# Attention scores from a head's own 64 rows in place of queries widened with zeros to 128 rows

## The chip, the cores and the metric

The kernel runs on one core of one Trainium2 chip. Its time is the device time of one execution in microseconds (us). The core has five engines that run side by side and wait for each other by semaphores: TensorE (PE, matrix products; its loads of stationary weights are listed apart as PEld), VectorE (DVE), ScalarE (ACT), GpSimd (POOL) and SyncE (SP, here only DMA issues).

## The reference

Two transformer blocks over 512 tokens of width 1024 are followed by a third block with a recurrence (RWKV-7) beside a convolution. The change touches only the attention of the first two. Every layer has 12 token heads and 4 memory heads of 64 channels:

```python
def windowed_gqa(q, k, v, sink, t5_table):       # layer 0: 12 query heads, 4 key heads
    ...
        s = jnp.einsum('bqkgd,bskd->bkgqs', q_blk, k_blk,
                       preferred_element_type=jnp.float32) * scale + bias
        s = jnp.where(valid, s, NEG)
        p = jax.nn.softmax(jnp.concatenate([s, sink_l], axis=-1), axis=-1)[..., :SPAN]
        return jnp.einsum('bkgqs,bskd->bqkgd', p.astype(v_blk.dtype), v_blk)

def neighbourhood_attn(q, k, v, rpb):            # layer 1: 12 heads on an 8x64 grid
    ...
        s = jnp.einsum('bwhd,brwchd->bhwrc', q_row, k_nb,
                       preferred_element_type=jnp.float32) * scale + bias
        p = jax.nn.softmax(s.reshape(B, B_HEADS, GRID_W, kr * kc), axis=-1)
        ...
        return jnp.einsum('bhwrc,brwchd->bwhd', p, v_nb)

def memory_attn(q, mk, mv):                      # both layers: 4 heads, 256 memory rows
    s = jnp.einsum('bshd,bmhd->bhsm', q, mk, preferred_element_type=jnp.float32) * (HEAD_DIM ** -0.5)
    p = jax.nn.softmax(s, axis=-1).astype(mv.dtype)
    return jnp.einsum('bhsm,bmhd->bshd', p, mv).reshape(B, S, MEM_HEADS * HEAD_DIM)
```

So each score is a sum over the 64 channels of one head. Layer 0 also takes a sink value per head into the softmax.

## The kernel before

All activations lie with channels on the 128 partitions (rows) and tokens along the free axis. A row tile of queries or keys holds two heads: one on rows 0 to 63, the other on rows 64 to 127. `qT` holds the token queries in 6 tiles, `kT` the keys, `qmT` the memory queries in 2 tiles, `mkT` the memory keys.

The program is written out engine by engine. Every engine runs its own list in order. For a dense layer ("project"), SyncE loads a panel of weights, ScalarE rounds it (w_hi, line L745), GpSimd forms the rest (w_lo, L602), and TensorE takes three passes per chunk of 128 channels (L1704, L1705, L1706). Two panels are in hand at a time. GpSimd's list has the two first panels of the output projection ahead of its work for attention (`split_lo(L["qm0"].p1 + 2)`, L607, and the same for layer 1 at L652).

Attention of one layer is 64 units: 8 tiles of two heads (the last two tiles are memory heads), times the two heads (e), times 4 blocks of 128 queries. A unit's keys are 128 x 2 or 3 wide in layer 0 (256 or 384), 192 or 256 in layer 1, and 256 for memory. For unit i:

- TensorE computes the score into PSUM (L1741): the stationary operand is the unit's queries, the moving one its keys. Both are fp32, and the trace shows two passes for such a product. It has to wait for the row maximum three units back.
- VectorE adds the bias (L1303) and takes the row maximum (L1309; L1300 without bias). In layer 0 GpSimd has put the sink beside the scores (`put_sink`, L619), and the maximum waits for it.
- ScalarE takes the exponential with its sum (L880).
- TensorE transposes the result (L1750), ScalarE copies that to pT (L854, L857), and TensorE multiplies it with the values (L1761, "PV").
- After 8 units the tile is normalised (L1283, L1284), turned to channels (L1727) and split for the output projection (L865, L1290).

TensorE's list interleaves these: score of unit i, transposes of unit i - 3, PV of unit i - 4, and so on. In layer 1 the windows of values are shifted by 64 keys, so that the first window of block 0 and the last of block 3 have 64 rows only (`pT[0:m, ...]` with m = 64); the trace shows their weights as `64*128`. The other weights of this loop have 128 rows, and a transpose with 64 columns appears as `128*64`.

The score of one head must not see the other head's rows. For that, GpSimd makes for every tile and both heads a copy of the 512 queries on 128 rows, the other head's rows multiplied by zero (`widen`, L621 to L626; the factor is a column of `head_ones`). The copies lie in `q_wide`, in the place of h_hi and h_lo. GpSimd widens tile t just before the sinks of tile t's units. The score of a tile's first unit waits for `q_wide_ready` (L1740).

Of the kernel before, what the change touches and what calls it, by code (L numbers as in the profile page):

```python
# [5 lines left out]
P = 128  # L6
D = 1024
KD = D // P
TOK = 512
NT = TOK // P  # L10
HD = 64
# [94 lines left out]
def build(nc, t, out, scratch):  # L106
# [4 lines left out]
    with ctx:  # L111
# [4 lines left out]
        sg = Signals()  # L116
# [59 lines left out]
        qT = at("qT", [P, 6, TOK], big)  # L176
        kT = at("kT", [P, 6, TOK], big + 12288)

        q_wide = at("q_wide", [P, 2, KD, TOK], h_off)
        qmT = at("qmT", [P, 2, TOK], big + 24576)  # L180
        vtok = at("vtok", [P, 5, HEADS * HD], big + 28672)
        bias_a = at("bias_a", [P, HEADS, SPAN_A], big + 44032)
# [130 lines left out]
        L = {}  # L313
# [21 lines left out]
        def units(layer):  # L335
            lst = []
            for tile in range(8):
                for e in range(2):
                    for blk in range(NT):
                        u = {"tile": tile, "e": e, "blk": blk, "sink": None, "bias": None}  # L340
                        u["q"] = q_wide[:, e, tile, blk * P:blk * P + P]
                        if tile >= 6:
                            b = 64 * e
                            u["from"] = (e, qmT[:, tile - 6, :])
                            u["k"] = mkT[:, layer, tile - 6, :]
                            u["w"] = MEM
                            vc = ((tile - 6) * 2 + e) * HD
                            u["v"] = [(i * P, P, mv[:, layer, i, vc:vc + HD]) for i in range(2)]
                        elif layer == 0:
                            head = 2 * tile + e  # L350
                            par, i = (head // 3) % 2, (head // 6) * 3 + head % 3
                            b = 64 * par
                            lo_k, hi_k = max(0, blk - 1), min(NT, blk + 2)
                            u["from"] = (par, qT[:, i, :])
                            u["k"] = kT[:, i // 3, lo_k * P:hi_k * P]
                            u["w"] = (hi_k - lo_k) * P
                            c0 = (lo_k - blk + 1) * P
                            u["bias"] = bias_a[:, head, c0:c0 + u["w"]]
                            u["sink"] = sinks[:, head:head + 1]
                            vc = (head // 3) * HD  # L360
                            u["v"] = [((i2 - lo_k) * P, P, vtok[:, i2, vc:vc + HD]) for i2 in range(lo_k, hi_k)]
                        else:
                            head = 2 * tile + e
                            b = 64 * e
                            s0, s1 = max(0, P * blk - 64), min(TOK, P * blk + 192)
                            u["from"] = (e, qT[:, tile, :])
                            u["k"] = kT[:, tile, s0:s1]
                            u["w"] = s1 - s0
                            c0 = s0 - (P * blk - 64)
                            ty = 0 if blk == 0 else (2 if blk == NT - 1 else 1)  # L370
                            u["bias"] = bias_b[:, head, ty, c0:c0 + u["w"]]
                            vc = head * HD
                            u["v"] = []
                            for w in (blk, blk + 1):
                                w0 = max(0, 128 * w - 64)
                                n = min(TOK, 128 * w + 64) - w0
                                u["v"].append((w0 - s0, n, vtok[0:n, w, vc:vc + HD]))
                        lst.append(u)
            return lst
# [202 lines left out]
        def _(pool):  # L582
# [26 lines left out]
            def attention(layer):  # L609
# [8 lines left out]
                        w = ul[i]["w"]  # L618
                        nc.gpsimd.tensor_copy(score[:, i % 4, w:w + 1], ul[i]["sink"]).then_inc(sg["sink_put"], 1)  # L619

                def widen(tile):  # L621

                    for e in range(2):
                        b, src = ul[8 * tile + 4 * e]["from"]
                        ins = nc.gpsimd.tensor_scalar(q_wide[:, e, tile, :], src, head_ones[:, 64 * b:64 * b + 1], None, ALU.mult)  # L625
                    ins.then_inc(sg["q_wide_ready"], 1)  # L626

                pool.wait_ge(used, last_reader[2 if layer == 0 else 5])
                for g in range(L[f"qm{layer}"].g0 + L[f"qm{layer}"].groups - 4, L[f"qm{layer}"].g0 + L[f"qm{layer}"].groups):
                    freed(pool, g)  # L630
                for i in range(NU):
                    if i % 8 == 0:
                        widen(i // 8)
                    put_sink(i)

            added = [0]
# [986 lines left out]
        def _(pe):  # L1623
# [92 lines left out]
            def attention(layer):  # L1716
# [15 lines left out]
                for i in range(NU + 4):  # L1732
                    if i < NU:
                        u = ul[i]
                        if i >= 3:
                            pe.wait_ge(sg["max_done"], b0 + i - 2)
                            if ul[i - 3]["bias"] is None:
                                pe.wait_ge(sg["exp_done"], b0 + i - 2)
                        if i % 8 == 0:
                            pe.wait_ge(sg["q_wide_ready"], 8 * layer + u["tile"] + 1)  # L1740
                        nc.tensor.matmul(ps[:, i % 3, 0:u["w"]], u["q"], u["k"], start=True, stop=True  # L1741
                                         ).then_inc(sg["s_done"], 1)
                    k = i - 3
# [415 lines left out]
```

## Time and profile before

| | us |
|---|---|
| median of 3 runs | 2575.73 (2573.24 to 2575.99) |
| profiled execution | 2571.74 |
| its span, first to last instruction | 2569.9 |
| TensorE busy | 2397.3 (93%) |
| ScalarE, VectorE, GpSimd busy | 901.2, 1022.1, 1031.3 |
| mean granted TensorE clock | 0.967 of 2.4 GHz |

A clock of 1.00 is 2.4 GHz, and 0.50 is the lower level, 1.2 GHz. Durations of matmuls include the time that a pass is under way inside the array, so that consecutive passes overlap in the trace; the distance between two starts tells the pace. Attention of layer 0 lies at about 146 to 256 us of the span and that of layer 1 at about 812 to 920 us. The transposes and products named above are all in these stretches.

### The profile page before, as it was taken

The page shows a single profiled execution, that of the slowest core. Times are in us where ns is not written, and L with a number is a line of the kernel's source. Part 1 is how long each engine was busy: PE and PEld are TensorE (multiplying, and loading weights), DVE is VectorE, ACT ScalarE, POOL GpSimd, SP SyncE. Part 2 cuts the span into 40 slices and gives each one's busy share as a digit, 9 for nine tenths or more (in the row PEclk, how much of TensorE's full clock was granted, in tenths as well). Part 3 has the DMA queues.
Part 4 walks back from the last instruction along what each step waited for, and adds up shares of the span by engine and source line. Part 5 has one row for each costly group of instructions (what it writes and reads, how often), then busy time and mean ns, then how long its engine had stood idle before and what let it go on. Part 6 is the DMA issues. An engine that isn't in the chain of part 4 may idle for free.

```text
span 2569.9 us, 41460 instructions
## 1 busy us (share of the span) xinstructions
PE 2397.3 (93%) x17520; PEld 1996.1 (78%) x17520; DVE 1022.1 (40%) x1492; ACT 901.2 (35%) x1519; POOL 1031.3 (40%) x594
## 2 busy tenths in 40 slices
PE   6889899999898989999988999999899998999998
PEld 6767678888687877888866888786888876788886
DVE  3246432221436643222125898437434445322212
ACT  3346433322413733222223222355233334332222
POOL 2342444444546044444454444434200244444444
PEclk9999999999899989999989999999899998999999
DMA  6510233333342022333333333322000222233332
GB/s 158 119 42 1 66 106 99 99 93 97 84 112 71 1 66 74 98 95 92 97 86 102 99 98 94 112 86 95 28 4 4 93 98 75 74 99 99 92 95 67
DMA packets 384265, 210.27 MB, mean 82 GB/s; under 512 B 36415, under 2 KB 378151, under 8 KB 383827
## 3 DMA queue, kind: packets, MB, share of 16 engines
q1 hardware_dynamic: 377340, 185.58, 25.7%
q0 software_dynamic: 4512, 18.09, 1.9%
q10 hardware_dynamic: 2231, 3.95, 0.5%
q8 instruction: 141, 2.31, 0.4%
q14 instruction: 41, 0.34, 0.0%
HBM read 196.72 MB, written 12.41 MB: 81 GB/s over the span
## 4 chain that ended last, share of the span: by engine, by line
PE 86%; POOL 4%; DVE 3%; issue 3%; ACT 2%; ACTq 0%; DMA 0%; POOLq 0%; DVEq 0%
PE ps L1704 23%; PE ps L1705 23%; PE ps L1706 23%; PE ps L2022 3%; PE ps L1741 2%; POOL x_res L644 2%; PE ps L1761 2%; PE ps L1989 2%; PE ps L2009 2%; PE ps L1750 1%; POOL q_wide L625 1%; POOL w_lo L602 1%; DVE h_lo L1185 1%; PE ps L2036 1%; ACT w_hi L745 1%
## 5 line engine op out<-in xcount | busy, mean ns | idle before, releaser
L602 POOL TENSOR_TENSOR w_lo<-raw,w_hi 128x1024 fp32r<-128x1024 f32 (+1 forms) x344 | 816.9, 2375 | 1124.7 <-ACT w_hi L745 1124.2
L1704 PE MATMUL ps<-h_hi,w_hi 128*128 128x512 f32 (+1 forms) x2144 | 852.3, 398 | 70.1 <-DVE h_lo L1185 28.0
L1705 PE MATMUL ps<-h_hi,w_lo 128*128 128x512 f32 (+1 forms) x2144 | 841.9, 393 | 0.0
L1706 PE MATMUL ps<-h_lo,w_hi 128*128 128x512 f32 (+1 forms) x2144 | 840.9, 392 | 0.0
L745 ACT ACTIVATE w_hi<-raw 128x1024 fp32r<-128x1024 f32 (+1 forms) x344 | 359.2, 1045 | 1213.7 <-PE ps L1706 1190.6
L1704 PEld LDWEIGHTS ps<-h_hi,w_hi 128*128 128x128 f32 x2144 | 412.3, 192 | 178.2 <-issue 91.2
L1706 PEld LDWEIGHTS ps<-h_lo,w_hi 128*128 128x128 f32 x2144 | 412.2, 192 | 85.3
L1705 PEld LDWEIGHTS ps<-h_hi,w_lo 128*128 128x128 f32 x2144 | 413.3, 193 | 80.6
L1706 PE MATMUL ps<-hid_lo,w_hi 128*128 128x512 f32 x528 | 205.4, 389 | 0.0
L1704 PE MATMUL ps<-hid_hi,w_hi 128*128 128x512 f32 x528 | 205.4, 389 | 0.0
L1705 PE MATMUL ps<-hid_hi,w_lo 128*128 128x512 f32 x528 | 205.4, 389 | 0.0
L1439 DVE SCALAR_TENSOR_TENSOR ps<-u_w,vecs,ps 128x511 f32<-128x511 f32 (+28 forms) x232 | 151.9, 733 | 0.0
L1158 DVE TENSOR_TENSOR h_sq<-h_sq 128x512 f32<-128x512 f32 x18 | 40.0, 2222 | 273.7 <-ACT h_sq L821 273.7
L1259 DVE TENSOR_TENSOR silu<-ps,spread_s 128x512 f32<-128x512 f32 x66 | 45.6, 691 | 250.1 <-PE ps L1706 250.0
L1265 DVE TENSOR_TENSOR hid<-ps,spread_s 128x512 f32<-128x512 f32 x66 | 45.6, 691 | 249.0 <-PE ps L1706 249.0
L1706 PEld LDWEIGHTS ps<-hid_lo,w_hi 128*128 128x128 f32 x528 | 99.1, 188 | 20.7
L1704 PEld LDWEIGHTS ps<-hid_hi,w_hi 128*128 128x128 f32 x528 | 99.1, 188 | 20.6
L1705 PEld LDWEIGHTS ps<-hid_hi,w_lo 128*128 128x128 f32 x528 | 99.1, 188 | 20.5
L1741 PE MATMUL ps<-kT,q_wide 128*128 128x256 f32 (+2 forms) x192 | 68.0, 444 | 20.8 <-POOL q_wide L625 20.8
L694 POOL TENSOR_TENSOR wk_lab_eye<-wk_lab_eye,masks 128x512 f32<-128x512 f32 x8 | 10.0, 1267 | 141.0 <-DVE wk_lab_eye L1555 141.0
L1761 PE MATMUL ps<-vtok,pT 128*128 128x64 f32 (+1 forms) x432 | 63.5, 269 | 0.1
L1761 PEld LDWEIGHTS ps<-vtok,pT 128*128 128x128 f32 (+1 forms) x432 | 57.4, 191 | 4.1 <-issue 1.8
(291 smaller groups left out, 2592.2 us busy)
## 6 DMA issues: line engine op xcount, KB each, us to landing
raw<-in_w_gu SPq DMA_DIRECT2D x88, 512.0 KB, 3.8
raw<-in_w_in SPq DMA_DIRECT2D x56, 512.0 KB, 3.8
raw<-in_w_down SPq DMA_DIRECT2D x32, 448.0 KB, 3.8
raw<-in_w_out SPq DMA_DIRECT2D x24, 512.0 KB, 4.2
raw<-in_ffn_w_gate SPq DMA_DIRECT2D x22, 512.0 KB, 3.8
raw<-in_ffn_w_up SPq DMA_DIRECT2D x22, 512.0 KB, 3.8
raw<-in_w_in_b SPq DMA_DIRECT2D x20, 512.0 KB, 4.0
raw<-in_w_down SPq DMA_DIRECT2D x16, 512.0 KB, 4.2
```

The lines of the kernel that those rows point to most:

```text
L602: nc.gpsimd.tensor_tensor(lo, src, hi.bitcast(f32), ALU.subtract).then_inc(lo_done, 1)
L644: nc.gpsimd.tensor_tensor(x_res[:, c, :], x_res[:, c, :], src[:, c, :], ALU.add).then_inc(sg["x_new"], 1)
L745: nc.scalar.activation(w_hi[p % 2][:, 0:pan.kc, :], raw[:, p % 4, 0:pan.kc, :], ACT.Copy).then_inc(hi_done, 1)
L1439: nc.vector.scalar_tensor_tensor(u_kk[:, c, s:TOK] if last else acc[:, s:TOK], u_w[:, c, 0:TOK - s], tap(TAPS - 1 - s, c), acc[:, s:TOK], ...
L1704: nc.tensor.matmul(ps[:, g % 4, 0:width], wh[:, k, :], ah, start=first, stop=False)
L1705: nc.tensor.matmul(ps[:, g % 4, 0:width], wl[:, k, :], ah, start=False, stop=False)
L1706: last = nc.tensor.matmul(ps[:, g % 4, 0:width], wh[:, k, :], al, start=False, stop=end)
L1741: nc.tensor.matmul(ps[:, i % 3, 0:u["w"]], u["q"], u["k"], start=True, stop=True).then_inc(sg["s_done"], 1)
L1761: last = nc.tensor.matmul(ps[:, 6 + u["tile"] % 2, c0:c0 + HD], pT[0:m, k % 3, j * P:(j + 1) * P], v, start=(j == 0), stop=(j == len(u["v" ...
L1989: last = nc.tensor.matmul(dst[side(block)], lhs, rhs, start=True, stop=True)
L2009: last = nc.tensor.matmul(ps[side(cb), bank, tile_of(h)], wk["lab_eye"][side(cb), h, :], wk["tri"][side(cb), h, :], start=True, stop=True)
L2022: last = nc.tensor.matmul(ps[side(cb), bank, tile_of(h)], a, b, start=True, stop=True)
```

## The change

The queries are no longer copied. The score takes as stationary operand the head's 64 rows of qT or qmT directly, and as moving operand the same 64 rows of the keys (`b` is 0 or 64). `q_wide`, `widen` and its waits go, and with them 16 GpSimd instructions per layer; the wait on `q_wide_ready` goes from TensorE's list.

```diff
@@ units @@
-                        u["q"] = q_wide[:, e, tile, blk * P:blk * P + P]
                         if tile >= 6:
                             b = 64 * e
-                            u["from"] = (e, qmT[:, tile - 6, :])
-                            u["k"] = mkT[:, layer, tile - 6, :]
+                            u["q"] = qmT[b:b + HD, tile - 6, blk * P:blk * P + P]
+                            u["k"] = mkT[b:b + HD, layer, tile - 6, :]
...
-                            u["from"] = (par, qT[:, i, :])
-                            u["k"] = kT[:, i // 3, lo_k * P:hi_k * P]
+                            u["q"] = qT[b:b + HD, i, blk * P:blk * P + P]
+                            u["k"] = kT[b:b + HD, i // 3, lo_k * P:hi_k * P]
...
-                            u["from"] = (e, qT[:, tile, :])
-                            u["k"] = kT[:, tile, s0:s1]
+                            u["q"] = qT[b:b + HD, tile, blk * P:blk * P + P]
+                            u["k"] = kT[b:b + HD, tile, s0:s1]
@@ GpSimd, attention @@
-                def widen(tile):
-
-                    for e in range(2):
-                        b, src = ul[8 * tile + 4 * e]["from"]
-                        ins = nc.gpsimd.tensor_scalar(q_wide[:, e, tile, :], src, head_ones[:, 64 * b:64 * b + 1], None, ALU.mult)
-                    ins.then_inc(sg["q_wide_ready"], 1)
-
-                pool.wait_ge(used, last_reader[2 if layer == 0 else 5])
-                for g in range(L[f"qm{layer}"].g0 + L[f"qm{layer}"].groups - 4, L[f"qm{layer}"].g0 + L[f"qm{layer}"].groups):
-                    freed(pool, g)
                 for i in range(NU):
-                    if i % 8 == 0:
-                        widen(i // 8)
                     put_sink(i)
@@ TensorE, attention @@
-                        if i % 8 == 0:
-                            pe.wait_ge(sg["q_wide_ready"], 8 * layer + u["tile"] + 1)
                         nc.tensor.matmul(ps[:, i % 3, 0:u["w"]], u["q"], u["k"], start=True, stop=True
                                          ).then_inc(sg["s_done"], 1)
```

GpSimd's list at the start of layer 0's attention before: the second panel of the output projection, then a tile's two widening instructions ahead of its sink copies (the last four are for memory heads, which have no sink).

```order
L602 TENSOR_TENSOR w_lo_73<-raw,w_hi_71 128x1024 [waits panel_used,w_hi_ready]
L625 TENSOR_SCALAR q_wide<-qT,head_ones 128x512 [waits bank_free1,bank_free2,bank_free0,bank_free3,panel_used,sink_loaded]
L625 TENSOR_SCALAR q_wide<-qT,head_ones 128x512
L619 COPY score<-sinks 128x1 x4
L619 COPY score<-sinks 128x1 [waits t_done] x4
...
L625 TENSOR_SCALAR q_wide<-qT,head_ones 128x512 x2
L619 COPY score<-sinks 128x1 [waits t_done] x8
L625 TENSOR_SCALAR q_wide<-qmT,head_ones 128x512 x4
L602 TENSOR_TENSOR w_lo_72<-raw,w_hi_70 128x1024 [waits panel_used,w_hi_ready]
```

The same place after:

```order
L600 TENSOR_TENSOR w_lo_73<-raw,w_hi_71 128x1024 [waits panel_used,w_hi_ready]
L617 COPY score<-sinks 128x1 [waits sink_loaded]
L617 COPY score<-sinks 128x1 x3
L617 COPY score<-sinks 128x1 [waits t_done] x44
L600 TENSOR_TENSOR w_lo_72<-raw,w_hi_70 128x1024 [waits panel_used,w_hi_ready]
```

All widening instructions are gone; the sink copies follow the panel at once. Line numbers have moved up by 2 here and by 16 in TensorE's list.

TensorE's list in layer 1, over the end of a tile, before: the score of one unit, transposes, the PV of a block 3 (its second product has 64 rows), then the score of the next tile's first unit.

```order
L1741 MATMUL ps<-kT,q_wide 128x192 [waits max_done]
L1750 MATMUL ps<-ident,score 64x128 [waits pt_ready,exp_done]
L1750 MATMUL ps<-ident,score 128x128
L1761 MATMUL ps<-vtok,pT 128x64 [waits pt_ready]
L1761 MATMUL ps<-vtok,pT 128x64
L1741 MATMUL ps<-kT,q_wide 128x192 [waits q_wide_ready,max_done]
```

The same place after:

```order
L1725 MATMUL ps<-kT,qT 128x192 [waits max_done]
L1734 MATMUL ps<-ident,score 64x128 [waits pt_ready,exp_done]
L1734 MATMUL ps<-ident,score 128x128
L1745 MATMUL ps<-vtok,pT 128x64 [waits pt_ready]
L1745 MATMUL ps<-vtok,pT 128x64
L1725 MATMUL ps<-kT,qT 128x192 [waits max_done]
```

No instruction moved; the score reads qT and has lost the wait for q_wide_ready. The rows show the shape of the result, so that the 64 rows of the operands don't appear in them.

## Rows read from the trace of the kernel before

**Rows 1.** The page, costliest groups: count, busy us, mean ns, idle before, releaser.

```profile
L1741 PE MATMUL ps<-kT,q_wide 128*128 128x256 f32 (+2 forms) x192 | 68.0, 444 | 20.8 <-POOL q_wide L625 20.8
```

**Rows 2.** Stretch; busy us (count) of PE, PEld, DVE, ACT, POOL; clock, DMA share, GB/s.

```profile
163.00:231.00 68.00, 59.58 (x416) 50.54 (x414) 46.57 (x98) 45.26 (x132) 25.70 (x54) 1.00 0.00 1
825.00:900.00 75.00, 74.52 (x511) 64.97 (x510) 48.09 (x123) 55.69 (x211) 15.56 (x11) 1.00 0.00 1
...
1872.00:2030.00 158.00, 144.80 (x4948) 140.89 (x4946) 61.50 (x93) 48.56 (x83) 9.99 (x8) 1.00 0.02 4
```

**Rows 3.** Waits of TensorE, 146 to 262 us: total, times, longest.

```profile
PE ps L1741 <- POOL q_wide L625: 15.4, 7, 6.8
```

**Rows 4.** Timeline at the start of layer 0: start, us, engine, idle before and releaser.

```profile
147.11 0.69 DVE L1206 SCALAR_TENSOR_TENSOR qmT<-ps,spread_s 128x512 f32<-128x512 f32 x1 [4.75 <-PE ps L1706]
...
150.64 3.10 POOL L625 TENSOR_SCALAR q_wide<-qT,head_ones 128x512 f32<-128x512 f32 x2
153.71 0.53 POOL L619 COPY score<-sinks 128x1 f32<-128x1 f32 x4
...
153.89 4.61 PE L1741 MATMUL ps<-kT,q_wide 128*128 128x256 f32 x8 [6.82 <-POOL q_wide L625]
...
155.65 0.42 DVE L1309 TENSOR_REDUCE row_max<-score 128x1 f32<-128x257 f32 x1
```

**Rows 5.** Timeline at the start of layer 1.

```profile
812.45 0.69 DVE L1206 SCALAR_TENSOR_TENSOR qmT<-ps,spread_s 128x512 f32<-128x512 f32 x1 [4.75 <-PE ps L1706]
...
819.16 3.33 PE L1741 MATMUL ps<-kT,q_wide 128*128 128x192 f32 x8 [6.82 <-POOL q_wide L625]
820.24 0.36 DVE L1303 TENSOR_TENSOR score<-ps,bias_b 128x192 f32<-128x192 f32 x1 [7.11 <-PE ps L1741]
```

**Rows 6.** Timeline of weight loads (PEld) in layer 1, 850.5 to 855.5 us.

```profile
850.88 0.36 PEld L1750 LDWEIGHTS ps<-ident,score 128*128 128x128 f32 x2
851.21 0.53 PEld L1761 LDWEIGHTS ps<-vtok,pT 128*128 128x128 f32 x4
851.65 0.30 PEld L1741 LDWEIGHTS ps<-kT,q_wide 128*128 128x128 f32 x2
...
853.03 0.30 PEld L1750 LDWEIGHTS ps<-ident,score 128*64 128x64 f32 x2
853.30 0.66 PEld L1761 LDWEIGHTS ps<-vtok,pT 128*128 128x128 f32 x4
854.03 0.30 PEld L1741 LDWEIGHTS ps<-kT,q_wide 128*128 128x128 f32 x2
854.30 0.30 PEld L1750 LDWEIGHTS ps<-ident,score 128*128 128x128 f32 x2
854.77 0.66 PEld L1761 LDWEIGHTS ps<-vtok,pT 64*128 64x128 f32 x4 [0.17 <-issue]
855.35 0.30 PEld L1741 LDWEIGHTS ps<-kT,q_wide 128*128 128x128 f32 x2
```

**Rows 7.** Timeline around 64-row products of 512 columns, TensorE, then two loads.

```profile
1764.34 0.39 PE L1706 MATMUL ps<-h_lo,w_hi 128*128 128x512 f32 x1
1764.65 2.84 PE L1884 MATMUL ps<-lora_wa,wa 64*128 64x512 f32 x6
...
1767.76 0.39 PE L1705 MATMUL ps<-h_hi,w_lo 128*128 128x512 f32 x1
1767.99 0.39 PE L1706 MATMUL ps<-h_lo,w_hi 128*128 128x512 f32 x1
...
1765.19 0.19 PEld L1884 LDWEIGHTS ps<-lora_wa,wa 64*128 64x128 f32 x1 [0.24 <-issue]
1765.62 0.19 PEld L1884 LDWEIGHTS ps<-lora_wa,wa 64*128 64x128 f32 x1 [0.24 <-issue]
```

**Rows 8.** Lines L1884 and L2082: minimum, median, maximum ns of a pass.

```profile
L1884 PE MATMUL ps<-lora_wa,wa x16: 589/589/694, 1756.2 to 1774.5; 64*128 64x512 f32 x16
...
L2082 PE MATMUL ps<-u_r,head_ones x16: 592/592/697, 2037.8 to 2057.8; 128*128 128x512 f32 x16
```

More of the change, by code:

```diff
@@ L177, in build @@
         kT = at("kT", [P, 6, TOK], big + 12288)
-        q_wide = at("q_wide", [P, 2, KD, TOK], h_off)
         qmT = at("qmT", [P, 2, TOK], big + 24576)
```

## The prediction, made before the change was run

> **What bounds the kernel now.** I read the page first. TensorE is busy for most of the span. The score line L1741 stands there with 192 matmul passes, 68.0 us busy and 20.8 us idle ahead of it, all of that idle time ended by GpSimd's q_wide, L625 [rows 1]. The same line has another 64 passes against the memory keys, so that it is 256 passes in all: 128 scores, each fp32 product in two passes. Then the windows: in the middle of layer 0's attention (163 to 231 us) TensorE is busy 59.58 of 68.00 us, in the middle of layer 1's (825 to 900 us) 74.52 of 75.00 us, against 48 and 56 us of VectorE and ScalarE there, at a granted clock of 1.00 [rows 2]. So attention runs at TensorE's pace, and whatever is put between two of its instructions is paid in full. In layer 0 some 8 us are lost beside that, and the waits say to whom: 15.4 us in 7 waits, the longest 6.8 us, on q_wide [rows 3]. The two starts show the long waits: 6.82 us of idle time each [rows 4, 5].
>
> **What the change removes.** Two widening instructions per tile, 3.10 us a pair, go from GpSimd [rows 4], and with them the wait of the score.
> (a) Six waits between tiles in layer 0: 15.4 - 6.8 = 8.6 us, 1.43 us each. GpSimd's next pair is queued behind sink copies that themselves wait for TensorE's transposes; without the pair the copies alone stay, far ahead of need. What is late next is nothing: TensorE was the engine that the others waited for. I take 8.6.
> (b) The start of layer 0. The first score could start when VectorE has written qmT, at 147.11 + 0.69 = 147.80 [rows 4]. But the row maximum includes the sink, and GpSimd copies it only after the weight panel that ends at 150.64. The four copies take 0.53, so the first is there by some 150.8, and allowing 0.1 for the signal the first maximum, now at 155.65, starts at 150.9. The gain is 4.75 us, not the 6 that the score itself moves.
> (c) The start of layer 1 has no sink. The score may start at 812.45 + 0.69 + 0.1 = 813.24 in place of 819.16: 5.9 us [rows 5]. The panel on GpSimd that stood ahead of the widening now hides nothing and holds nobody. Beside it the idle time ahead of the score shrinks from 6.82 us to about one, so that the first scores may run at 2.4 GHz instead of 1.2; VectorE starts 1.08 us after the first score began [rows 5], so this is worth between 0 and 1.1 us. I take 0.5.
> Sum of the gains: 8.6 + 4.75 + 5.9 + 0.5 = 19.75 us, take 19.8.
> Waits on bank_free that GpSimd drops cost and gain nothing: what follows on it, the fourth out panel and on, waits for TensorE anyhow.
>
> **What it adds.** The number and order of TensorE's instructions stay. But a score now loads 64 rows of weights, between PV products and transposes that load 128. Half the rows are not half the time: 64x512 of L1884 and 128x512 of L2082 both have fp32 medians near 0.59 us [rows 8]. So nothing is gained inside the score. The question is what it costs to go between the two heights, and layer 1 does that already, in the PV products of a tile's first and last block, where one window has 64 keys. By weight loads [rows 6]:
> - Ordinary block: PV from 851.21 to the score's load at 851.65: 0.44 us.
> - Last block (two loads of 128 rows, two of 64, then the score at 128): 853.30 to 854.03: 0.73 us. Two changes of height, 0.29 us extra.
> - First block: the transposes take 854.30 to 854.77, 0.47 us against 851.21 - 850.88 = 0.33 ordinary: 0.14 for the change to 64. Its PV takes 854.77 to 855.35, 0.58 against 0.44: 0.14 for the change back.
> So a change of height costs 0.14 us behind narrow matmuls. Behind wide ones: L1706 starts at 1764.34, six 64-row passes follow at 0.43 each (1765.62 - 1765.19), and L1705 starts at 1767.76 [rows 7]. Without a cost it were 1764.34 + 0.23 + 6 x 0.43 + 0.23 = 1767.38 (0.23 is the pace of the 128-row passes, from L1705 at 1767.76 to L1706 at 1767.99). The 0.38 left over is two changes, 0.19 each.
> In the changed kernel a score is entered behind narrow PV products: 0.14. It is left behind passes of 192 to 384 columns at their full rate: between 0.14 and 0.20; I take 0.17, the middle, as neither neighbour is of its width.
> Count per layer: scores 0 to 3 follow each other. Scores 4 to 63 are entered from 128 rows, 60 entries; scores 3 to 63 are left, 61 exits. In layer 1, 12 scores follow a last block's PV, whose last load has 64 rows already: these 12 entries are free, and the 12 changes that this place has now go too.
> Sum: (60 + 48) x 0.14 = 15.1; 122 x 0.17 = 20.7; minus 12 x 0.14 = 1.7; that is 34.1 us. At each start a few changes fall into time in which TensorE waits for the first exponential; for these I take off 1 us. Cost 33.1 us.
> **Net: 33.1 - 19.8 = 13.3 us slower.** The profiled execution took 2571.74 us (span 2569.9), 4 us under the median of the three runs, 2575.73. So I get 2585.0 on its basis and 2589 on the median's, which I forecast. With exits at 0.14 and 0.20 the net is +9.6 and +17.0.
> The cost needs nothing hidden: in 825 to 900 us TensorE has half a microsecond idle.
>
> The direction is one for which the Trainium skill has a rule: TensorEngine Tiling (Array Packing), section Key Properties, says that changing the tiling mode, not merely the tile, drains TensorE. It gives no time. For the change of rows the rows above agree (0.14 to 0.19 us). For a change of columns they do not: transposes whose first has 64 columns take from 853.03 to 853.30, 0.27 us, less than the ordinary 0.33 [rows 6]. So the rule in its full width is not what I sum with. It lowers the chance that I give below to a free exit.
> The skill's TensorE: Matmul & The Clock Gate, section on packing small matmuls, says that products on different row groups run concurrently. Here that could help only where 64-row loads of different halves meet, 6 of the 12 places in layer 1; at most the narrowing of these by a score pass each. It would change the sum by under 3 us.
>
> **Rivals.**
> 1. The change of height costs nothing around a score: the costs in [rows 6] would belong to the mixed pair inside one accumulation, not to the height. Then only the gains stay: 2575.7 - 19.8 = 2556, faster. For it: all narrow examples lie in or next to such a pair. Against it: L1884 of [rows 7] is no such pair and pays the same. 6 in 100.
> 2. The exit is free and the entry is not: the transposes' loads, hidden under a wide score pass now, stay hidden. Cost 15.1 - 1.7 = 13.4, net -6.4: 2569. Against it: leaving the wide passes in [rows 7] was not free. It decides by whether a transpose's load starts before the score's second pass has ended. 8 in 100. Something between this and the forecast, at 2572 to 2580: 6 in 100.
> 3. The waits between tiles in layer 0 are replaced: a score waits for the maximum of three units before, since VectorE serves it later. Then (a) is lost: 2589 + 8.6 = 2598. VectorE's 46.57 us busy of 68 speak against it [rows 2]. 5 in 100.
> 4. The clock falls, as half the array is idle in each score and TensorE stands more. The recurrence stage of 64x64 products keeps 1.00 over 158 us [rows 2], which speaks against it. If it fell for a tenth of the 143 us of [rows 2], 14 us of work would take 28: 2603. 2 in 100.
> My forecast has 73 in 100.
>
> **How the numbers follow.** The measurement tells 0.2%, 5.2 us, from no change: faster is under 2570.6, slower over 2580.9. Faster holds rivals 1 and 2, 0.13 (rival 2 lies just at the border). Same holds the rest of rival 2 and most of the middle: 0.07. Slower 0.80. The forecast's own range is 2584 to 2594; the one for 8 in 10 reaches from 2573 (into the middle case) to 2598 (rival 3).
>
> **What would show it.** (1) The row L1741 <- POOL is gone, and the score's starts follow VectorE's qmT by 0.1 us in both layers. (2) Steady units in layer 1 with 128-row PV take some 0.31 us more from one score's load to the next than before; (3) the load of the first transpose starts about 0.1 us after the score's second pass has ended instead of under it, and idle time of PEld appears ahead of both. (4) The score behind a 64-row PV shows no step. (5) Score passes keep their durations (mean 444 ns against keys in [rows 1]). (6) Attention at 1.00 clock. If units keep their length, rival 1 is right and the forecast wrong; if only entries show a step, rival 2.

## The result: 6.3% slower, at half the TensorE clock through attention

The changed kernel took 2739.72 us (median of 4 runs, 2732.36 to 2743.50) against 2575.86 us (2573.24 to 2580.19): ratio 1.0631, 95% interval [1.0601, 1.0660]. The forecast of 2589 us, range 2573 to 2598, had the sign and missed the size: +164 us instead of +13.

The page of the changed kernel, the score line (answer to [rows 1]; L1725 was L1741):

```profile
L1725 PE MATMUL ps<-kT,qT 64*128 64x256 f32 (+2 forms) x192 | 117.0, 713 | 3.4 <-DVE qmT L1192 2.0
```

The wait on GpSimd is gone (20.8 us of idle time are now 3.4, on VectorE), but a pass takes 713 ns in the mean where it took 444. Nothing in the program doubles a pass. The windows say what did (stretch, busy us and count of PE, PEld, DVE, ACT, POOL, then the granted clock, DMA share, GB/s). Attention of layer 0 and of layer 1, changed kernel, answer to [rows 2]:

```profile
146.00:345.00 199.00, 194.88 (x630) 134.75 (x629) 65.65 (x137) 68.25 (x202) 10.87 (x49) 0.52 0.02 6
903.00:1066.00 163.00, 160.80 (x537) 111.35 (x536) 53.53 (x132) 59.78 (x224) 0.71 (x1) 0.50 0.01 4
```

The kernel before, over its own two attention stages, starts included:

```profile
146.00:256.00 110.00, 93.52 (x624) 78.97 (x623) 64.38 (x137) 68.62 (x202) 35.21 (x65) 0.96 0.04 11
812.00:920.00 108.00, 99.21 (x612) 84.71 (x611) 56.69 (x138) 66.48 (x232) 31.75 (x19) 0.94 0.05 15
```

0.50 is 1.2 GHz. The two stages now stand almost wholly at the lower level. Measured from the last product of the qm projection to the first of the output projection, layer 0's stage takes 195.0 us (147.32 to 342.34) where it took 107.9 (146.68 to 254.61), and layer 1's 166.4 (899.73 to 1066.16) where it took 92.0 (811.95 to 903.91): 87.1 + 74.4 = 161.5 us. The stretch between them is 557.4 us now and 557.3 before. Of the remaining 10 us of the 171.8 between the two spans, 9.6 lie behind layer 1's attention (1675.5 us there against 1666.0). No run traced them to a cause; the two profiled executions lie 3.8 us over and 4.1 us under the medians of their kernels, so that 7.9 us of the 171.8 are spread between executions.

The start shows where the clock goes. Windows of the changed kernel around layer 0's start:

```profile
150.00:152.00 2.00, 0.65 (x3) 0.04 (x1) 0.47 (x2) 0.00 (x0) 1.78 (x5) 1.00 0.00 0
152.00:154.00 2.00, 1.24 (x3) 0.52 (x3) 1.93 (x5) 1.96 (x4) 0.00 (x0) 0.50 0.67 198
154.00:156.00 2.00, 2.00 (x5) 1.02 (x6) 0.95 (x4) 1.88 (x7) 0.18 (x1) 0.50 0.22 65
```

And of the kernel before:

```profile
154.00:156.00 2.00, 2.00 (x4) 1.37 (x5) 0.77 (x2) 0.00 (x0) 0.24 (x3) 0.50 0.02 7
...
158.00:160.00 2.00, 1.89 (x10) 1.44 (x8) 1.90 (x6) 1.78 (x7) 0.33 (x2) 0.75 0.00 0
160.00:162.00 2.00, 2.00 (x15) 1.69 (x16) 1.08 (x3) 1.58 (x6) 0.22 (x2) 1.00 0.00 0
```

Both fall to 0.50 at the start of attention, after TensorE has been partly or wholly idle. The kernel before is back at 1.00 at some 159 us, five microseconds into its units. The changed one never comes back in that stage, although its busy column shows no idle time: from 160 to 340 us every ten microseconds show PE busy 10.00. The durations in that column overlap, so that it can't show short stops between passes; the idle time of the loads below shows them.

One unit of the changed kernel, by its weight loads (PEld, start and duration in us; answer to [rows 6], in layer 0, score of 384 columns):

```profile
206.92 0.50 PEld L1725 LDWEIGHTS ps<-kT,qT 64*128 64x128 f32 x2
208.50 0.50 PEld L1734 LDWEIGHTS ps<-ident,score 128*128 128x128 f32 x3 [1.08 <-issue]
208.98 1.40 PEld L1745 LDWEIGHTS ps<-vtok,pT 128*128 128x128 f32 x6
210.50 0.50 PEld L1725 LDWEIGHTS ps<-kT,qT 64*128 64x128 f32 x2
```

From one score's load to the next: 3.58 us (206.92 to 210.50). And the transposes' load stands 1.58 us behind the score's, with 1.08 us of idle time: it no longer runs under the score's passes. The same kind of unit before:

```profile
206.47 0.30 PEld L1741 LDWEIGHTS ps<-kT,q_wide 128*128 128x128 f32 x2
206.91 0.14 PEld L1750 LDWEIGHTS ps<-ident,score 128*128 128x128 f32 x1
...
207.45 0.75 PEld L1761 LDWEIGHTS ps<-vtok,pT 128*128 128x128 f32 x6
208.12 0.30 PEld L1741 LDWEIGHTS ps<-kT,q_wide 128*128 128x128 f32 x2
```

1.65 us (206.47 to 208.12), and the first transpose's load starts 0.44 us behind the score's, under its passes.

### The profile page after: what moved, and what is told of

It is laid out like the page before. It is cut to its first block, busy times and chain, and to the rows that moved or that the text cites. A ratio compares the mean times of both kernels' runs of the same rounds, so it can differ in the third digit from the quotient of the medians.

```text
span 2741.7 us, 41409 instructions
## 1 busy us (share of the span) xinstructions
PE 2588.0 (94%) x17520; PEld 2100.7 (77%) x17520; DVE 1024.4 (37%) x1492; ACT 900.3 (33%) x1519; POOL 982.1 (36%) x562
## 4 chain that ended last, share of the span: by engine, by line
PE 88%; DVE 4%; POOL 3%; issue 3%; ACT 2%; ACTq 0%; DMA 0%; POOLq 0%; DVEq 0%
PE ps L1690 21%; PE ps L1691 21%; PE ps L1692 21%; PE ps L1725 5%; PE ps L1745 4%; PE ps L1734 3%; PE ps L2006 3%; POOL x_res L630 2%; PE ps L1973 1%; PE ps L1993 1%; DVE h_lo L1171 1%; POOL w_lo L600 1%; ACT w_hi L731 1%; PE ps L2020 1%; PE ps L1713 1%
## 5 line engine op out<-in xcount | busy, mean ns | idle before, releaser
L1725 PE MATMUL ps<-kT,qT 64*128 64x256 f32 (+2 forms) x192 | 117.0, 713 | 3.4 <-DVE qmT L1192 2.0
L1745 PEld LDWEIGHTS ps<-vtok,pT 128*128 128x128 f32 (+1 forms) x432 | 105.1, 330 | 7.2 <-issue 3.9
L1745 PE MATMUL ps<-vtok,pT 128*128 128x64 f32 (+1 forms) x432 | 108.3, 404 | 0.0
L1734 PEld LDWEIGHTS ps<-ident,score 128*128 128x128 f32 (+1 forms) x280 | 41.5, 203 | 85.8 <-issue 73.0
```

The source lines that it names most:

```text
L1734: last = nc.tensor.transpose(ps[0:m, 3 + k % 3, j * P:(j + 1) * P], score[:, k % 4, off:off + m], ident[:, :])
L1745: last = nc.tensor.matmul(ps[:, 6 + u["tile"] % 2, c0:c0 + HD], pT[0:m, k % 3, j * P:(j + 1) * P], v, start=(j == 0), stop=(j == len(u["v" ...
```

## The experiments

All times are medians beside runs of the kernel before on the same chip (2573.4 to 2575.2 us); ratios are to those. C stands for "changes of height keep the clock low", H for "half height as such does", S for "the shorter, changed start loses it".

**1. The score's operands alone.** q_wide and its waits stay:

```diff
+ u["q"] = q_wide[b:b + HD, e, tile, blk * P:blk * P + P]
- u["k"] = kT[:, tile, s0:s1]
+ u["k"] = kT[b:b + HD, tile, s0:s1]
```

> GpSimd still widens and TensorE still waits for q_wide; only the score's operands are cut to 64 rows. In the changed kernel the granted clock is 0.50 through both attention stages. Theory R (the 64-row score itself keeps the clock at 1.2 GHz): 0.50 here too from the start to the end of attention, and about 2740 us; the six waits of 1.4 us vanish under the slower TensorE. Theory S (the new, shorter start is what leaves the clock low; the old start with 6.8 us of idle time does not): clock 1.00 after the start as before, and 2575.9 + 33 = 2609 us.

Measured: 2748.55 us, 1.0671 [1.0650, 1.0692].

```profile
150.00:345.00 195.00, 190.46 (x610) 131.26 (x611) 63.53 (x133) 66.75 (x200) 34.49 (x65) 0.50 0.01 3
```

Layer 1 stands at 0.51 from 905 to 1068 us. The operands' height does it with the old start in place, so theory S isn't needed for the loss; the next run shows that the new start doesn't suffice for it.

**2. The other part alone.** No widening, scores over 128 rows of qT and kT (`u["q"] = qT[:, tile, ...]`, `u["k"] = kT[:, tile, ...]`). The scores then sum two heads, so that this kernel leaves out the separation of the heads; its instructions are those of full height.

> The other part alone: no widening, but the score takes all 128 rows of queries and keys, so that it sums the products of two heads (this part of the computation is changed). Theory R: clock 1.00 in attention, and the gains of the prediction alone: 2575.9 - 19.8 = 2556 us (2554 to 2560). Theory S: clock 0.50 as in the changed kernel, over 2650 us.

Measured: 2552.3 us, 0.9911 [0.9891, 0.9932], 22.9 us under before. The interval reaches from 17.5 to 28.1 us and holds the predicted 19.8. Of the waits left for TensorE in layer 0 these are the score's (total us, times, longest):

```profile
PE ps L1725 <- DVE row_max L1295: 1.4, 1, 1.4
...
PE ps L1725 <- DVE qmT L1192: 1.0, 1, 1.0
```

No wait took the place of the removed ones: four waits, 4.7 us in all, are left in 146 to 262 us, and between 162 and 252 us a single one of 1.0 us, behind VectorE's tok_out. The clock at this start:

```profile
154.00:158.00 4.00, 3.55 (x13) 2.96 (x14) 2.13 (x5) 3.34 (x12) 0.37 (x2) 0.50 0.22 65
158.00:162.00 4.00, 4.00 (x20) 3.24 (x19) 1.60 (x3) 1.47 (x4) 0.37 (x2) 0.64 0.00 0
162.00:166.00 4.00, 4.00 (x31) 3.49 (x30) 2.92 (x8) 3.02 (x10) 0.56 (x3) 1.00 0.00 0
```

So with the new, shorter start the clock falls too, and a loop of full height climbs out again, as the kernel before does. Runs 1 and 2 together put the loss down to the 64-row scores.

**3. The changed kernel, started warm.** Fillers in TensorE's idle time, 4 before score 3 in layer 0 and 1 in layer 1, and 3 behind it:

```diff
+ def busy(n):
+     for _ in range(n):
+         nc.tensor.matmul(ps[:, 7, :], ident[:, :], x_res[:, 0, :], start=True, stop=True)
+ if i == 3: busy(4 if layer == 0 else 1)
...
+ if i == 3: busy(3)
```

> The changed kernel with filler products (128x512, 128 rows, into an unused bank) in the idle time at the start of each attention, so that the clock has not fallen when the units begin. If a low clock at the start only can't be left again (theory S, or a form of R in which the loop holds a high clock but can't regain it): 1.00 through attention, and the predicted 2589 us or a little more (up to 2595). If the loop can't hold a high clock (theory R in full): the clock falls within some microseconds of the last filler, and 2735 to 2745 us.

Measured: 2622.31 us, 1.0182 [1.0161, 1.0204]; three of the four runs within 1 us. The fourth took 2661.83 us at a mean clock of 0.937 against 0.949 to 0.954, so that the clock isn't held equally long in every execution. Layer 0, then layer 1 in two stretches:

```profile
150.00:268.00 118.00, 116.98 (x656) 81.30 (x655) 64.68 (x136) 70.35 (x202) 10.36 (x49) 1.00 0.02 5
830.00:866.00 36.00, 36.00 (x215) 25.54 (x213) 22.73 (x59) 25.47 (x92) 0.00 (x0) 1.00 0.00 1
868.00:950.00 82.00, 82.00 (x280) 57.64 (x279) 24.28 (x58) 29.81 (x109) 0.00 (x0) 0.50 0.00 1
```

The same loop runs at 1.00 or at 0.50: layer 0 kept the clock that it was given for 118 us, and layer 1 lost it at 867 us with TensorE busy 2.00 of every 2.00 us around the fall by the busy column. So both parts of the expectation came true, one in each layer. With this run the cost of a change of height can be read at full clock, in layer 0:

```profile
207.59 0.29 PEld L1731 LDWEIGHTS ps<-kT,qT 64*128 64x128 f32 x2
208.42 0.31 PEld L1742 LDWEIGHTS ps<-ident,score 128*128 128x128 f32 x3 [0.55 <-issue]
208.70 0.75 PEld L1753 LDWEIGHTS ps<-vtok,pT 128*128 128x128 f32 x6
209.52 0.29 PEld L1731 LDWEIGHTS ps<-kT,qT 64*128 64x128 f32 x2
```

1.93 us from score to score, against 1.65 before, for the same unit: 0.28 us for two changes. The forecast summed 0.31. Other units agree: the most frequent distance between two scores is 1.39 us against 1.10 before, in both layers while the clock is 1.00.

**4 and 5. One short product more per unit, of 64 rows or of 128,** ahead of a full-height score (kernel before):

```diff
+ nc.tensor.matmul(ps[:, i % 3, 448:449], qT[0:64, 0, 0:P], kT[0:64, 0, 0:1], start=True, stop=True)   # 4
+ nc.tensor.matmul(ps[:, i % 3, 448:449], qT[:, 0, 0:P], kT[:, 0, 0:1], start=True, stop=True)         # 5
```

> The kernel before with one additional product of 64 rows and one column ahead of each 128-row score. This puts two changes of height into each unit and leaves the score at full height. If the changes of height (TensorE standing between them) are what keeps the clock low: 0.50 through attention, over 2750 us. If it is the score at half height: clock 1.00, and 128 x (two loads at 0.107 + two changes at 0.14) = 63 us more than before, 2639 us (2625 to 2660).

> The control of the run with an additional 64-row product: the same product with 128 rows, one column, no change of height. That run had the clock at 0.50 for 45 us of layer 0 and for most of layer 1. Theory C (the changes of height keep the clock low): here 1.00 after the start as in the kernel before, and 128 x 2 loads x 0.107 = 27 us more than before, 2603 us (2595 to 2612). Rival (any two short products more per unit keep it low): over 2680 us.

Measured: with 64 rows 2725.15 us, 1.0582 [1.0550, 1.0615] (three runs within 8 us, one at 2764.88); with 128 rows 2616.16 us, 1.0150 [1.0113, 1.0188] (2599.40 to 2618.90). Windows of the 64-row run:

```profile
160.00:200.00 40.00, 40.00 (x136) 32.04 (x136) 13.65 (x28) 13.25 (x39) 6.15 (x15) 0.50 0.00 0
200.00:300.00 100.00, 95.43 (x613) 81.10 (x612) 49.61 (x104) 54.52 (x160) 23.32 (x44) 1.00 0.01 1
860.00:1000.00 140.00, 139.62 (x488) 115.50 (x488) 44.12 (x111) 48.39 (x172) 21.81 (x15) 0.50 0.00 1
```

and of the 128-row run:

```profile
170.00:197.00 27.00, 26.85 (x124) 22.48 (x123) 11.26 (x24) 11.44 (x32) 4.98 (x13) 0.62 0.00 0
200.00:320.00 120.00, 114.43 (x718) 98.85 (x718) 58.38 (x98) 63.58 (x165) 36.79 (x44) 1.00 0.09 27
840.00:870.00 30.00, 30.00 (x111) 25.81 (x112) 10.04 (x26) 12.35 (x42) 21.06 (x14) 0.50 0.00 1
```

Full-height scores with changes of height stay at the low clock too: until 200 us in layer 0 and, in layer 1, until 1048 us, the end of the stage (1000 to 1048 us show 0.50 as well). The control isn't clean, against what I expected of it. Without a change of height the same two short passes leave the clock at 0.50 for some 20 us in layer 0 (170 to 190 us, behind a wait of 1.5 us on q_wide; the kernel before has a like wait of 1.7 us there and stays at 1.00) and for the first 33 us of the units in layer 1 (840 to 873). So a short 64-row product per unit keeps the clock low for longer than one of 128 rows, but a change of height isn't needed for it.

**6. A burst in the middle:** six fillers ahead of the score of unit 16.

> The changed kernel with one burst of 6 filler products (128 rows, 512 columns) ahead of unit 16 of each layer, no filler at the start. With the warm start layer 0 held 1.00 to its end and layer 1 for 45 us. Theory C with two states (the loop cannot regain the high clock by itself, but holds it when given): 0.50 up to the burst, 1.00 for long behind it in layer 0, a part of layer 1; a low-clock unit costs 1.1 to 1.5 us more, so that 48 units of layer 0 and some of layer 1 give back 75 to 115 us, less 16 us for the bursts: 2640 to 2685 us. Rival (only the moment of the start counts, or the loop falls at once): 2740 to 2760 us.

Measured: 2630.48 us, 1.0224 [1.0169, 1.0280] (2618.74 to 2647.08), better than expected.

```profile
160.00:190.00 30.00, 30.00 (x95) 20.11 (x94) 9.74 (x20) 9.61 (x29) 1.66 (x9) 0.50 0.00 1
200.00:310.00 110.00, 108.98 (x607) 80.89 (x607) 55.57 (x104) 61.58 (x168) 15.29 (x35) 1.00 0.06 18
840.00:870.00 30.00, 28.65 (x93) 18.96 (x92) 11.85 (x31) 12.57 (x47) 1.44 (x1) 0.51 0.06 18
880.00:920.00 40.00, 40.00 (x231) 27.74 (x230) 24.78 (x63) 27.05 (x95) 0.00 (x0) 1.00 0.00 1
930.00:970.00 40.00, 40.00 (x139) 28.79 (x139) 9.77 (x22) 14.40 (x50) 0.00 (x0) 0.50 0.00 0
```

The burst brings the clock back both times. Layer 0 then keeps it to its end, and layer 1 loses it again after some 50 us, as in run 3, and has it at 0.50 to the end of its stage.

**7. Scores in pairs:** units i and i + 1 together, half as many changes, the same 64-row work:

```diff
+ if i < NU and i % 2 == 0:
+     score_of(i)
+     score_of(i + 1)
```

> The changed kernel with the scores of units i and i + 1 next to each other, so that half as many changes of height are left (about 30 scores per layer entered and left in place of 60) and the 64-row work is the same. Theory C: fewer stops, so that the loop may regain the clock after the start; then 2576 - 19.8 + 16 = 2572 us, at best. If half the changes are still too many: 0.50 through attention and 30 to 40 us less than the changed kernel, 2700 to 2710 us. Rival H (the half-height score as such keeps the clock low): 0.50 through both layers.

Measured: 2674.85 us, 1.0411 [1.0346, 1.0477] (2665.84 to 2703.55).

```profile
160.00:230.00 70.00, 70.00 (x242) 53.32 (x242) 27.07 (x56) 25.10 (x77) 4.44 (x24) 0.50 0.00 1
240.00:280.00 40.00, 40.00 (x261) 31.59 (x260) 24.32 (x53) 26.16 (x88) 2.40 (x13) 1.00 0.00 1
850.00:990.00 140.00, 139.29 (x501) 108.86 (x502) 51.49 (x127) 55.91 (x216) 0.00 (x0) 0.50 0.01 4
```

The time lies between my two cases: the loop regained the clock by itself, at some 235 us in layer 0, but not before 993 us in layer 1, where the last PV product is at 995 us. With half the changes layer 0 comes back by itself; with all of them it never did.

**8. Full height, widened early.** GpSimd makes the first tile's copies between the last panels, into a place of its own, and each later tile's in two halves one tile ahead:

```diff
+ wide = q_wide[:, e, tile, :] if tile else q_first[:, e, :]
...
+ for e in range(2):
+     split_lo(L[f"qm{layer}"].p0 + 1 + e)
...
+     widen(layer, 0, e)
...
-                    if i % 8 == 0:
-                        widen(i // 8)
                     put_sink(i)
+                    if i % 8 in (3, 6) and i < NU - 8:
+                        widen(layer, i // 8 + 1, int(i % 8 == 6))
```

> The kernel before, scores of 128 rows and q_wide kept, but GpSimd widens earlier: tile 0 between the last panels ahead of attention into a place of its own, each further tile in two halves during the tile before it. No wait for q_wide should be left. The kernel without any widening took 2552.3 us (0.9911 of before). Expected: the same gains, 2556 us (2551 to 2560), clock 1.00 from some microseconds after the start. If GpSimd's load during projections or the sinks behind a widening cost time: 2560 to 2570 us.

Measured: 2555.48 us, 0.9930 [0.9907, 0.9953]. The gain was to be had without touching TensorE's products.

**9 and 10. Half height without changes, and its full-height counterpart.** In the first, scores, transposes and PV products all take rows 0 to 63, the latter two twice over; in the second the same instructions take 128 rows.

```diff
+ for r in (0, 64):
+     last = nc.tensor.transpose(ps[0:m, 3 + k % 3, j * P + r:j * P + r + 64],
+                                score[0:64, k % 4, off:off + m], ident[0:64, 0:64])
```

> Half height without changes of height: scores, transposes and PV products all take 64 rows, always rows 0 to 63, and each transpose and PV product is issued twice (the values computed are those of the lower half only). No idle time is put between heights, but never more than half the array is at work. Theory C (what keeps the clock low is that TensorE stands at changes of height): 1.00 from some microseconds after the start; by loads, a unit of 128x256 has 14 in place of 8, 0.107 us each, part of it under the score's passes, so some 0.4 us more per unit than without widening: about 2600 us (2590 to 2630). Theory H (half height as such): 0.50 through attention, over 2720 us.

> The counterpart at full height: no widening, scores, transposes and PV products of 128 rows (scores sum two heads, PV products are added twice, so the values computed differ), the latter two issued twice as in the run at half height; only the short windows of layer 1 keep their 64 rows. Both theories: 1.00 after the start, about 2600 us (2590 to 2630). What it and the run at half height differ in is what half height costs alone.

Measured: half height 2814.12 us, 1.0935 [1.0917, 1.0953]; full height 2636.57 us, 1.0240 [1.0220, 1.0261]. Half height:

```profile
160.00:370.00 210.00, 210.00 (x926) 182.23 (x926) 54.59 (x114) 58.04 (x170) 7.58 (x41) 0.50 0.00 1
```

Full height:

```profile
158.00:300.00 142.00, 140.98 (x1083) 128.76 (x1083) 60.49 (x126) 66.95 (x193) 9.33 (x43) 1.00 0.01 1
820.00:930.00 110.00, 107.33 (x728) 94.57 (x726) 58.48 (x129) 54.05 (x182) 13.01 (x6) 1.00 0.10 30
```

Theory C as the sole cause falls here: no changes of height, TensorE busy 210.00 of 210.00 us, and 0.50 all the way. The two runs differ in one thing more than height: each transposing pass has 64 columns in the half-height run (`64x64`) and 128 in the other (`128x128`). So the half-height loop has shorter passes too, and run 5 shows that short passes alone can cost the clock for a while. The full-height run took 6.6 us more than the top of its expectation with the clock at 1.00: against run 2 the doubling cost 84 us, 0.66 us per unit, where I had 0.4.

**11. Half height throughout, started warm** (the fillers of run 3, two and two).

> The run at half height throughout (values of the lower half only, 2814 us, 0.50 through attention), with fillers of full height in the idle time of each start. If half height holds a clock that it is given, as the mixed loop does: 1.00 through attention and about 2640 us (2625 to 2660). If half height as such drops it: 0.50 within microseconds of the fillers, 2805 to 2825 us.

Measured: 2810.80 us, 1.0912 [1.0891, 1.0933].

```profile
154.00:158.00 4.00, 4.00 (x32) 2.81 (x31) 1.68 (x5) 2.86 (x10) 0.37 (x2) 1.00 0.02 5
162.00:380.00 218.00, 218.00 (x965) 189.63 (x964) 55.99 (x118) 60.30 (x179) 7.44 (x40) 0.50 0.00 1
```

The loop at half height throughout can't even keep the clock: 1.00 under the fillers, 0.50 from about 160 us. The mixed loop of run 3 could in layer 0.

**12. Pairs, started warm.**

> 64-row scores in pairs (half as many changes), with short fillers in the idle time of each start. Pairs alone took 2674.9 us, their clock came back after 85 us in layer 0 and after 145 us in layer 1. Theory C with two states: given the high clock at the start, both layers keep it, and 2576 - 19.8 + 16 = 2572 us (2568 to 2580). Rival (layer 1 falls on the way, as with the unpaired scores): 2600 to 2640 us.

Measured: 2565.36 us, 0.9968 [0.9954, 0.9981].

```profile
150.00:250.00 100.00, 98.98 (x618) 75.49 (x617) 63.44 (x135) 63.73 (x200) 10.73 (x49) 1.00 0.02 7
812.00:895.00 83.00, 81.98 (x537) 65.27 (x536) 51.16 (x127) 55.53 (x220) 0.00 (x0) 1.00 0.02 7
```

64-row scores at 1.00 in both layers, and 9 us under the kernel before; the 2572 us expected from the forecast's terms were 7 us too many, and no run shows which term.

**13 and 14. Pairs in opposite halves,** without and with fillers. The units' order is turned, so that a tile's two heads follow each other:

```diff
-                for e in range(2):
-                    for blk in range(NT):
+                for blk in range(NT):
+                    for e in range(2):
```

> Paired scores without fillers, but with the two heads of a tile following each other, so that a pair's 64-row scores lie in opposite halves in layer 1, the memory tiles and two of six token tiles of layer 0 (in the others both heads use one half). If two halves run beside each other, a pair takes one score's time: 0.43 to 0.6 us less in 48 of 64 pairs; and the array stands at full height again, so that the clock may come back sooner than the 85 and 145 us of the same-half pairs (2674.9 us): 2560 to 2640 us. If halves don't overlap: 2665 to 2700 us, as the pairs.

> The same with the short fillers at each start. Pairs of one half with fillers took 2565.4 us at a high clock. If opposite halves overlap: 48 pairs x 0.43 to 0.6 = 20 to 27 us less, 2542 us (2536 to 2550), which would also beat the full-height version with early widening (2551.0). If they don't overlap: 2565 us.

Measured: without fillers 2573.74 us, 1.0008 [0.9988, 1.0028] (ten runs, 2570.79 to 2592.77); with fillers 2548.39 us, 0.9897 [0.9882, 0.9913]. A pair with fillers, opposite halves, on TensorE in layer 1:

```profile
846.05 0.70 PE L1730 MATMUL ps<-kT,qT 64*128 64x256 f32 x4
846.68 0.44 PE L1746 MATMUL ps<-ident,score 128*128 128x128 f32 x2
```

and of one half (run 12):

```profile
845.60 1.02 PE L1730 MATMUL ps<-kT,qT 64*128 64x256 f32 x4
846.55 0.44 PE L1746 MATMUL ps<-ident,score 128*128 128x128 f32 x2
```

Four passes of 256 columns take 0.63 us to the next transpose in place of 0.95. 0.32 us in 48 pairs are 15 us, and the medians are 17.0 us apart. The clock without fillers (the profiled execution took 2592.43 us, 19 us over the median, so that other executions may have had the high clock for longer):

```profile
160.00:180.00 20.00, 20.00 (x83) 15.77 (x82) 8.21 (x19) 8.85 (x26) 1.67 (x9) 0.50 0.00 1
190.00:250.00 60.00, 60.00 (x420) 47.25 (x418) 41.59 (x90) 42.35 (x137) 5.38 (x29) 1.00 0.01 2
820.00:885.00 65.00, 65.00 (x269) 49.52 (x268) 28.30 (x74) 29.31 (x117) 0.00 (x0) 0.50 0.02 4
```

Back at some 185 us in layer 0 (pairs of one half: 235) and at some 890 us in layer 1 (one half: not before 993 us, the end of its stage).

**15. Full height, widened early, one filler before and one behind score 3.**

> Full-height scores, widening put early (2555.5 us), and one filler product of two passes before and one behind score 3 in each layer, in TensorE's idle time. The clock should not fall at the start, so that the 5 to 8 us of low clock there, worth 2 to 3 us per layer, go: 2551 us (2547 to 2556). If the fillers delay the first transposes as much as the clock gives back: 2555 to 2558 us.

Measured: 2551.02 us, 0.9907 [0.9893, 0.9922]. 4.5 us less than version 8 for two fillers per layer, though the intervals of the two ratios overlap (0.9907 to 0.9953 there), so that the runs don't tell them apart for certain.

The fastest is version 14, 2548.39 us and 1.03% under the kernel before, with version 15 at 0.93%; their intervals overlap.

## Why the prediction was wrong

**The step that failed** is the one on the clock: rival 4 ("The clock falls, as half the array is idle in each score and TensorE stands more"), with 2 in 100 and 2603 us, and point (6) of what would show the forecast right, "Attention at 1.00 clock". The mechanism was named and then priced for a tenth of 143 us. What the runs showed in its place: 0.50 for nearly all of some 360 us. Between the 2589 us forecast with the clock at 1.00 and the 2739.7 measured lie 151 us. Run 3 shows 81 of them directly: with the clock at 1.00 layer 0's stage takes 113.9 us instead of 195.0. For layer 1 no run kept this loop at 1.00 to its end.

**The evidence against it was misread.** I put the recurrence stage of 64x64 products at 1.00 [rows 2] against a fall. That stage issues products of both halves in turn (its loops run over both sides), and so does not show what one half alone does. Runs 9 and 11 do: one half alone, no idle time in the busy column, 0.50. With scores of both halves in turn (run 13) the clock came back sooner than with pairs of one half (run 7): at 185 against 235 us, and at 890 against 993 us.

**The start was not looked at for its state.** The kernel before falls to 0.50 in each attention start and climbs out within some five microseconds. That climb is an event that the change could take away, and the 64-row scores did (runs 1 and 2). I priced the clock at the start at 0 to 1.1 us of gain, and counted no chance that the low clock would simply last. Run 3 (same loop, warm start, 1.00 in layer 0) is what the forecast was about.

**The terms of the sum stood.**
- GpSimd's part: 19.8 us forecast, 22.9 measured (run 2, 17.5 to 28.1).
- Changes of height: 0.31 us per unit forecast, 0.28 measured at full clock (run 3). By the loads, from the score's to PV's is 1.11 us against 0.98, 0.13 for leaving, and from PV's to the next score's 0.82 against 0.67, 0.15 for entering; for the exit I had 0.17, with 0.14 as its lower bound.
- Layer 0 in run 3: 60 x 0.14 + 61 x 0.14 = 16.9, less 13.35 for its share of the gains, gives +3.6. The fillers held the first transpose back until 157.94 us; in the changed kernel it starts at 153.98, with a stage that begins 0.43 us earlier, so that this costs up to 3.5. That is +3.6 to +7.1. Measured from the last product of the qm projection to the first of the output projection, the stage took 113.9 us (147.75 to 261.63) against 107.9 before: +6.0.

The Trainium skill has the rule that a change of tiling mode drains TensorE (TensorEngine Tiling (Array Packing), Key Properties). It agrees with the 0.55 us of idle load time behind the score at full clock and the 0.28 us per unit (run 3). The Trainium skill also says that small products placed in different parts of the array run concurrently (TensorE: Matmul & The Clock Gate, Part 3: Packing small matmuls). That agrees with 0.63 against 0.95 us (run 14 against 12). I had noted the latter as worth under 3 us, as the order of the units gave it no neighbours; the order could be changed.

**Rivals.** 1 (changes cost nothing) and 2 (free exit) fall by run 3: both entering and leaving cost time. 3 (waits replaced) falls by run 2.

**What stays open.** That 64-row scores between full-height products keep the clock low is shown (1, 2); why they do is not. Half height throughout, with shorter transposing passes (9, 11), a 64-row product beside full-height scores (4), and for a while a short product of full height (5) all lower the clock or keep it low. Whether these are one cause or several, the runs don't tell. Why layer 1 loses a clock that layer 0 keeps (runs 3, 6) isn't settled either; its scores are narrower, 192 or 256 columns against 256 or 384, which was not tried alone. And the changes' direct cost inside the low clock can't be taken apart from the clock here.

## What to carry to other kernels

- Before cutting a product's rows, read the granted clock where the loop starts. Where it falls there and recovers, a leaner loop may never recover: a median of +164 us here, for a step priced at +13.
- TensorE can show busy 10.00 of 10.00 us at half speed. Look at the clock column of the windows before the busy column.
- 64-row products gained something here only in pairs whose neighbours lie in opposite halves, with fillers at the start (version 14), and even so the kernel is not told apart from version 15 with full-height scores; between 128-row products one alone costs 0.28 us. A few filler products in an idle start were worth some 4.5 us at full height, if anything, and 25 to 117 us where 64-row scores stand between full-height products (runs 14 against 13, 12 against 7, 3 against the changed kernel). Where everything had half height the medians are 3 us apart and the intervals of the ratios overlap.

## What the runs showed of the hardware

- The same loop of 64-row scores ran at two speeds: 1.93 us (run 3) and 3.58 us (changed kernel) for a unit of 384 columns. In layer 0 the clock that it entered with decided which one held for the whole stage; in layer 1 the high one lasted some 50 us. A burst of 6 fillers brought it back in the middle (run 6).
- The clock fell with no idle time in the busy column: run 3 at 867 us, run 11 at 160 us.
- Going from 128-row to 64-row weights and back around a score of 384 columns cost 0.28 us at full clock (run 3). Products with 64-row weights in opposite halves overlapped: four passes of 256 columns took 0.63 instead of 0.95 us to the next transpose (runs 14 and 12).
